# Heads sweep: up-projections as three float32r products in place of float32 products

## The reference

```python
MLA_HEADS, MLA_NOPE, MLA_ROPE, MLA_V = 4, 64, 32, 64      # MLA_QK = 96
MLA_Q_RANK, MLA_KV_RANK = 192, 128

def mla_queries(q_lat, q_norm_g, w_uq, q_head_g, rope):
    q = (rms_norm(q_lat, q_norm_g) @ w_uq).reshape(b, L, MLA_HEADS, MLA_QK)
    q = rms_norm(q, q_head_g)
    ... # rotary positions on the last 32 channels

def mla_keys(ckv, krope, w_ukv, k_head_g, rope):
    kv = (ckv @ w_ukv).reshape(b, L, MLA_HEADS, MLA_NOPE + MLA_V)
    k_nope, v = kv[..., :MLA_NOPE], kv[..., MLA_NOPE:]
    ...

    # in each layer, u = normalised input @ w_in
    ckv = rms_norm(a_kv, prm['mla_kv_norm_g'][l])
    q_a = mla_queries(a_q, prm['mla_q_norm_g'][l], prm['mla_w_uq'][l], ...)
    k_a, v_a = mla_keys(ckv, a_r, prm['mla_w_ukv'][l], ...)
```

## Time and profile before

| | us |
|---|---|
| median of 3 runs (3946.63 to 3953.41) | 3950.85 |
| the profiled execution, its span | 3950.6 |

### The profile page before, as it was taken

One profiled execution on the slowest core, in us unless ns is written; L12 is line 12 of the kernel. 1 busy time (PEld: TensorE's weight loads), 2 busy tenths in 40 slices (PEclk: granted clock), 3 DMA queues, 4 the chain that ended last, 5 costly groups with the idle time before them and its releaser, 6 DMA issues. The chain is left out here.

```text
span 3950.6 us, 51229 instructions
## 1 busy us (share of the span) xinstructions
PE 3646.9 (92%) x18304; PEld 2578.0 (65%) x18304; DVE 2875.2 (73%) x5006; ACT 1502.9 (38%) x3066; POOL 177.5 (4%) x263
## 2 busy tenths in 40 slices
PE   6799989959999999998969999895889999999899
PEld 1798878736566555556869978784655655555587
DVE  1555979959677778876745489786877777888676
ACT  0661114456334344442136411343933343444411
POOL 0000000000000000001100000000010000100010
PEclk8899999968899999998989999997979999999899
DMA  7654547652222222204456354576142211230243
GB/s 301 180 176 142 175 145 186 178 140 69 33 66 66 44 45 44 45 21 143 171 159 198 130 171 164 163 196 182 48 89 47 66 34 33 61 61 12 75 170 138
DMA packets 340870, 450.83 MB, mean 114 GB/s; under 512 B 134152, under 2 KB 272776, under 8 KB 323744
## 3 DMA queue, kind: packets, MB, share of 16 engines
q1 hardware_dynamic: 323424, 324.62, 26.7%
q0 software_dynamic: 17216, 123.22, 12.0%
HBM read 291.64 MB, written 156.10 MB: 113 GB/s over the span
## 5 line engine op out<-in xcount | busy, mean ns | idle before, releaser
L2142 ACT ACTIVATE attn_Pb<-attn_ST 128x1024 f32<-128x1024 f32 x544 | 547.4, 1027 | 878.8 <-PE attn_ST L2024 518.8
L2168 DVE TENSOR_REDUCE attn_mx<-attn_p 128x1 f32<-128x1024 f32 x496 | 607.4, 1225 | 271.6 <-PE attn_p L1965 264.4
L2212 DVE TENSOR_TENSOR attn_acc<-attn_acc,attn_Pb 128x1024 f32<-128x1024 f32 x480 | 583.9, 1216 | 29.9 <-ACT attn_Pb L2142 28.5
L2036 PE MATMUL attn_OT<-attn_Pb,attn_V 128*64 128x512 f32 x2176 | 549.1, 619 | 0.0
L604 PE MATMUL chan_b<-w_in_turned,w_in_hi 128*128 128x256 f32 (+1 forms) x1152 | 326.5, 283 | 0.0
L605 PE MATMUL chan_b<-w_in_turned,w_in_lo 128*128 128x256 f32 (+1 forms) x1152 | 324.7, 282 | 0.0
L606 PE MATMUL chan_b<-chan_hl,w_in_hi 128*128 128x256 f32 (+1 forms) x1152 | 323.3, 281 | 0.0
L924 DVE SCALAR_TENSOR_TENSOR gate_GY<-gate_win,w_in_fw,gate_GY 128x1096 f32<-128x1096 f32 x240 | 310.8, 1352 | 0.4
L2036 PEld LDWEIGHTS attn_OT<-attn_Pb,attn_V 128*64 128x64 f32 x2176 | 130.2, 138 | 227.8 <-issue 194.7
L888 PE MATMUL gate_b<-w_in_hi,w_in_turned 128*128 128x512 f32 x544 | 216.8, 398 | 17.9 <-PEq L461 17.9
L2377 PE MATMUL out_pY<-ahead_hi,out_oTh 128*128 128x512 f32 x544 | 221.2, 407 | 0.0
(11 more groups left out here) (370 smaller groups left out, 7221.8 us busy)
## 6 DMA issues: line engine op xcount, KB each, us to landing
w_in_turned<-scratch_HT POOLq DMA_DIRECT2D x68, 1024.0 KB, 5.4
mod_w<-in_w_mod SPq DMA_DIRECT2D x16, 1536.0 KB, 11.5
scratch_HT<-w_in_turned SPq DMA_DIRECT2D x34, 512.0 KB, 3.7
scratch_HT<-chan_hl SPq DMA_DIRECT2D x34, 512.0 KB, 4.7
scratch_G<-gate_GT SPq DMA_DIRECT2D x34, 512.0 KB, 2.9
out_G<-scratch_G SPq DMA_DIRECT2D x30, 512.0 KB, 4.9
scratch_QM<-head_QST SPq DMA_DIRECT2D x34, 384.0 KB, 3.8
scratch_KM<-head_KST SPq DMA_DIRECT2D x34, 384.0 KB, 5.0
```

The lines of the kernel that those rows point to most:

```text
L2036: mm = pe.matmul(OT[o * HD:(o + 1) * HD, :], V[par][:, kt, :], Pb[unit % NPB][:, o * 512:(o + 1) * 512], start=(kt == 0), stop=(kt == NKT ...
L2142: act.activation(Pb[unit % NPB][:, :], ST[unit % 2][:, :], ACT.Exp).then_inc(q["exp_done"], 1)
L2168: ins = dve.tensor_reduce(mx[:, t, w:w + 1], made[:, :], AX.X, ALU.max)
L2212: ins = dve.tensor_tensor(sums[:, :], sums[:, :], prob[:, :], ALU.add)
```

## The change

The latents' copy LT becomes a high part LTh (written by ScalarE as float32r) and a low part LTl = bL - LTh (two subtractions by VectorE in the new `latent_low`). The two weights are split once at the start of the stage, the high parts by ScalarE, the low parts by VectorE. The up-projections become nine float32r products for three float32 ones. TensorE waits for the low parts (`lt_low`) after the products that need only high parts, and it also waits for them before it writes bL anew.

```diff
@@ -973,7 +973,9 @@
         ck = s.sb("ck", [P, KVR])
-        LT = s.sb("LT", [P, 3, P])
+        LTh, LTl = s.sb("LTh", [P, 3, P], F32R), s.sb("LTl", [P, 3, P], F32R)
+        uqh, uql = s.sb("uqh", [QK, 2, 4 * QK], F32R), s.sb("uql", [QK, 2, 4 * QK], F32R)
+        ukvh, ukvl = s.sb("ukvh", [P, 4 * P], F32R), s.sb("ukvl", [P, 4 * P], F32R)
         qsq = s.sb("qsq", [P, 4, QK])
@@ -992,7 +994,7 @@
                  "norm_steps qlck_ready q_steps qk_ready qkr_ready g_steps gn_ready gr_ready "
-                 "dt_stored0 dt_stored1 v3_stored0 v3_stored1 v_stored q_stored k_stored g_stored out_stored").split()
+                 "up_high up_low lt_low dt_stored0 dt_stored1 v3_stored0 v3_stored1 v_stored q_stored k_stored g_stored out_stored").split()
         q = {n: s.sem(n) for n in names}
@@ -1085,13 +1087,19 @@
-                    pe.wait_ge(q["small"], 32 + START)
+                    pe.wait_ge(q["up_low"], 2 + START)
                     pe.wait_ge(q["lt_ready"], n + START)
...
                     for a in range(2):
-                        pe.matmul(bU[:, 0:4 * QK], LT[0:QK, a, :], wuq[:, a, :], start=(a == 0), stop=(a == 1))
-                    pe.matmul(bK[:, :], LT[:, 2, :], wukv[:, :], start=True, stop=True).then_inc(q["s2_done"], 1)
+                        pe.matmul(bU[:, 0:4 * QK], LTh[0:QK, a, :], uqh[:, a, :], start=(a == 0), stop=False)
+                        pe.matmul(bU[:, 0:4 * QK], LTh[0:QK, a, :], uql[:, a, :], start=False, stop=False)
+                    pe.matmul(bK[:, :], LTh[:, 2, :], ukvh[:, :], start=True, stop=False)
+                    pe.matmul(bK[:, :], LTh[:, 2, :], ukvl[:, :], start=False, stop=False)
+                    pe.wait_ge(q["lt_low"], n + START)
+                    for a in range(2):
+                        pe.matmul(bU[:, 0:4 * QK], LTl[0:QK, a, :], uqh[:, a, :], start=False, stop=(a == 1))
+                    pe.matmul(bK[:, :], LTl[:, 2, :], ukvh[:, :], start=False, stop=True).then_inc(q["s2_done"], 1)
                 if n >= 2:
@@ -1109,7 +1117,7 @@
                     pe.wait_ge(q["qlck_ready"], n + 1 + START)
-                    pe.wait_ge(q["lt_ready"], n + START)
+                    pe.wait_ge(q["lt_low"], n + START)
                     for a in range(2):
@@ -1119,6 +1127,9 @@
+            act.wait_ge(q["small"], 32 + START)
+            act.activation(uqh[:, :, :], wuq[:, :, :], ACT.Copy)
+            act.activation(ukvh[:, :], wukv[:, :], ACT.Copy).then_inc(q["up_high"], 1)
             for n in range(NT + 2):
@@ -1154,8 +1165,8 @@
                     act.wait_ge(q["s2_done"], n + START)
-                    act.activation(LT[0:QK, 0:2, :], bL[0:QK, 0:2 * P], ACT.Copy)
-                    act.activation(LT[:, 2, :], bL[:, 2 * P:3 * P], ACT.Copy).then_inc(q["lt_ready"], 1)
+                    act.activation(LTh[0:QK, 0:2, :], bL[0:QK, 0:2 * P], ACT.Copy)
+                    act.activation(LTh[:, 2, :], bL[:, 2 * P:3 * P], ACT.Copy).then_inc(q["lt_ready"], 1)
@@ -1195,6 +1206,12 @@
                 dve.scalar_tensor_tensor(ck[:, :], e[:, A_KV:A_R], r[:, 1:2], gkv[:, :], ALU.mult, ALU.mult).then_inc(q["qlck_ready"], 1)
+
+            def latent_low(n):
+
+                dve.wait_ge(q["lt_ready"], n + 1 + START)
+                dve.tensor_tensor(LTl[0:QK, 0:2, :], bL[0:QK, 0:2 * P].rearrange("p (a t) -> p a t", a=2), LTh[0:QK, 0:2, :].bitcast(F32), ALU.subtract)
+                dve.tensor_tensor(LTl[:, 2, :], bL[:, 2 * P:3 * P], LTh[:, 2, :].bitcast(F32), ALU.subtract).then_inc(q["lt_low"], 1)
@@ -1216,6 +1233,8 @@
                 dve.tensor_tensor(QKt[:, :, NOPE:QK], m1[:, :, :], m2[:, :, :], ALU.add).then_inc(q["qkr_ready"], 1)
+                if m + 1 < NT:
+                    latent_low(m + 1)
@@ -1242,11 +1261,16 @@
+            dve.wait_ge(q["up_high"], 1 + START)
+            dve.tensor_tensor(uql[:, :, :], wuq[:, :, :], uqh[:, :, :].bitcast(F32), ALU.subtract).then_inc(q["up_low"], 1)
+            dve.tensor_tensor(ukvl[:, :], wukv[:, :], ukvh[:, :].bitcast(F32), ALU.subtract).then_inc(q["up_low"], 1)
             for n in range(NT + 2):
...
                     latents(n)
+                if n == 0:
+                    latent_low(0)
                 if 1 <= n <= NT:
```

## The result

The changed kernel takes 3960.75 us (median of 15 runs, 3957.96 to 3964.23), the kernel before, run beside it, 3952.01 us: 8.7 us slower by the medians. The ratio is 1.0024, with an interval of 1.0017 to 1.0030, which is 9.5 us and 6.7 to 11.9 for the interval. The profiled execution has a span of 3959.9 us against 3950.6.

The account below looks back on a forecast made before the run. TensorE was taken as the bound (98% busy), VectorE close behind; afterwards a 13.42 us circuit plus 0.10 late copies sets the tile. +6.0 us for 28 tiles and +2.1 for starts make +8.1, forecast 3959 us, range 3952 to 3967.

Parts of the forecast that it names:

- The products: TensorE's up-projections from bU to the next bQ: 1.75 us instead of 2.16, 0.41 us less a tile.
- The low parts: VectorE's two latent subtractions out of PSUM each tile: 0.55 us, or an estimated 0.65 by the skill page.
- The circuit: Heads sweep loop from bQ through latents' copy, subtractions and KST back to bQ: 13.42 us, longer than either engine's work.
- Late copies: Delays of ScalarE's latents' copy add whole to the tile: 0.10 us a tile, ends 0 and 0.30.
- the bare circuit: The 13.42 us loop of a heads-sweep tile without late copies, against 13.305 us a tile before.
- The start: VectorE's weight split (1.47 us) delays the first bL by 1.32 us; each layer starts 1.05 us late, both +2.1.
- The sum of +8.1: Whole predicted change: +6.0 us for 28 even heads-sweep tiles plus +2.1 us for both layers' starts.
- TensorE's share alone: Rival: TensorE's work sets the sweep's time, so the change gains 10.5 us, 3940 us; chance 0.04.
- VectorE's sum: Rival: VectorE's work of 13.20 us a tile decides, without the circuit; -0.8 us, 3950 us; chance 0.09.
- Late copies as the larger part: Rival: late latents' copies average 0.30 us, tile 13.72 us, +13.7 us, 3964.5 us; decides from 0.2; chance 0.17.

Follow-up runs that it names:

- the products alone: Changed kernel without the latents' subtractions, the three low-part products reading the high part instead; 3945.08 us, ratio 0.9989 to the kernel before.
- the low parts alone: Kernel before, products still float32, with only VectorE's two latent subtractions a tile and their waits added; 3959.99 us, ratio 1.0026.
- GST moved: Changed kernel with ScalarE's copy into GST, which waits for the previous tile's store, placed behind the latents' copy; 3952.94 us, ratio 1.0008.
- the last one: Changed kernel with keys' squares before KV, weights' split and most latent subtractions later, and keys' rotary scaling on GpSimd; 3942.05 us, ratio 0.9981.
- the weights' split moved: Changed kernel with VectorE's split of the two weights behind the first tile's latents instead of ahead of the first means; 3957.19 us, ratio 1.0021.

## Why the prediction was right

Forecast 3959 us, measured 3960.75. Its steps one by one.

- *The products*: bU's start to the end of the last bK product's slot was to be 1.75 us. In the even tiles of the products alone in which TensorE has no wait in front of bQ, bU's start to bQ is 1.74 to 1.78. Right.
- *The low parts* at 0.55 us by start-to-start times: 762.34 - 761.80 = 0.54. The dearer pair that the Trainium skill (VectorE: DVE Perf Modes, TRN2 errata) would give, an estimated 0.65, isn't in this trace.
- *The circuit* of 13.42 us: 13.39 to 13.40 wherever the copy is on time, and in all 28 tiles with the wait for the store moved. VectorE no longer waits 0.60 us ahead of the queries' reduction (767.66 - 767.52 = 0.14), it waits for the copy; TensorE waits 0.40 in front of bQ (0.5 had been named). Right; the low parts alone show that what takes the saving does not depend on the products.
- *Late copies*, 0.10 us a tile: this is the term that was mis-sized. They measured 0.35 and 0.17, 0.26 in the mean; 28 x 0.16 = 4.5 us more than allowed, offset by the bare circuit's 0.03 x 28 = 0.8 and so leaving +9.6 where +6.0 stood. Of the 9.6, 7.1 are late copies and 2.4 the bare circuit, where the sum had 2.8 and 3.2. The reason given, that a longer tile leaves the stores more time, fails by the rows: the store of GST goes out behind L1261, which ends 0.32 us after bQ (739.01 in the late tile), and the latents' copy is on time when GST's copy starts within 6.3 us of that end, else late by the excess (7.58 in the late tile, 1.27 late). The store's issue and the latest punctual start of the copy both hang on bQ, so the store has 6.3 us however long the tile is. The first stretch thereby left the 187.9 to 190 us that had been named.
- *The start*: the split took 567.53 - 566.06 = 1.47 us as worked out, and the first bL moved by 1.02 and 1.43 where 1.32 stood; the second bQ by 0.72 and 1.18 (1.05). The sum of 2.1 came out (1.9), the reason holds only for the first layer; in the second it is luck. Over the ten traces the first bL comes at the later of two times: 5.60 us after TensorE's first bD product, or 3.04 after VectorE's first instruction of the means.

```
us after the weights' load   first bD   first means   first bL
before, layer 1                 6.93        9.26        12.53
after, layer 1                  7.00       10.52        13.55
before, layer 2                 5.54        7.98        11.14
after, layer 2                  6.96        8.54        12.57
GST moved, layer 2              5.62        8.42        11.45
```

In layer 2 the gains land 1.3 us (before) and 2.0 us (after) sooner than in layer 1, so VectorE has room: the split costs nothing there in the changed kernel (8.54 + 3.04 = 11.58, a microsecond ahead of TensorE) and 0.2 us with GST moved. What came 1.43 later was TensorE's own bD, by its clock (last section).
- *The rest of the program* was taken as unchanged; in this pair of profiles it was 2.2 us shorter and hid most of the mis-sized term. The sum of +8.1 stands against +11.5 in the two stages that it was worked out for, +9.3 in the spans of the profiles and +8.7 by the medians (+9.5 by the ratio). That the time came as close as 3959 to 3960.75 is in part luck.

Of the rivals, TensorE's share alone fell with the float32r products run alone (13.10, not 12.84), VectorE's sum with the 13.40 of punctual tiles. Late copies as the larger part came in by the prediction's own bound, a mean delay of 0.2 us or more: 0.26, with 13.65 us a tile in the mean, between the forecast's 13.52 and that rival's 13.72. The mechanism was the forecast's, its size in the tiles was the rival's. Why stores are late more often in some kernels than in others (0.07 us a tile in the last one, 0.32 with the weights' split moved, with the same stores in both) was not tried and stays open.

## What to carry to other kernels

Before work is added to a second engine, follow the added wait until it comes back to where it started: if the circle is longer than every engine's own work, a saving outside it is worth nothing, and every irregular wait inside it is paid in full. Look then for what stands in the circle without need: here an instruction that waits for a store stood ahead of the copy that everyone waits for, and exchanging the two gave back most of the loss in the tiles. And a start seen in one layer isn't the other's: look at which engine leads in each.

## What the hardware showed

TensorE's clock explains the scatter of the starts. It enters the stage after 10.1 to 10.4 us without work, the first products run at the lower of its two levels (0.50, which is 1.2 GHz), and when the clock rises to 1.00 (2.4 GHz) differs. The first 7 us of layer 2, after:

```profile
2492.40:2499.40 7.00, 6.77 (x25) 6.80 (x25) 0.41 (x3) 1.37 (x2) 0.00 (x0) 0.55 0.65 155
```

and before:

```profile
2485.60:2492.60 7.00, 6.80 (x31) 6.56 (x32) 0.07 (x1) 1.22 (x7) 0.00 (x0) 0.78 0.59 156
```

In the one the clock stayed at 0.50 for the first 6 us, in the other for 3; the same 24 products took 1.4 us longer. Over the twenty starts of the ten traces these products take from 5.3 us (clock 0.78 in the first 7 us) to 6.8 (0.54 to 0.56), and late and early rises occur with and without the change. A pause inside the sweep's start can do the same: with the low parts behind the GQA heads TensorE waited 2.25 us for VectorE in front of the first layer's first bL,

```profile
569.00 0.66 PE L1122 MATMUL head_bL<-ident,head_ql 128*96 128x128 f32 x2 [2.25 <-DVE head_ck L1208]
```

by stretch (columns as in the earlier trace rows, the clock third from the end)

```profile
570.00:572.00 2.00, 2.00 (x8) 2.00 (x8) 1.08 (x3) 0.46 (x2) 0.00 (x0) 0.50 1.01 377
574.00:578.00 4.00, 4.00 (x22) 3.61 (x21) 0.00 (x0) 2.41 (x10) 0.00 (x0) 1.00 0.02 1
```

and ran the next products at 1.2 GHz before it came back to 2.4. In the products alone a pause of 2.32 us did likewise (0.50 from 570 to 572 us), and with GST's copy moved one of 2.20 us, where the second bQ of the first layer came 2.1 us later than before; after the changed kernel's 0.80 us the clock stayed at 1.00. The three long pauses stand behind early rises: TensorE was through its first work sooner, and VectorE, with the weights' split ahead of its means, was not.
